# Convolution norm by streamed squares in channel layout, and q and k of head pair 1 by block products in a seventh front round

## What is computed

```python
h = rms_norm(x, g_pre_mix[l])
proj = jnp.einsum('bsd,dp->bsp', h, w_in[l])
hc, bg, cg, q, k, v = jnp.split(proj, 6, axis=-1)      # 512 columns each
y_conv = short_gated_conv(hc, bg, cg, w_conv[l])       # bg * conv3(cg * hc)
y_attn = chunked_band_attention(q, k, v, rel_bias[l])  # 8 heads of 64
y = jnp.concatenate([group_rms_norm(y_conv, g_conv_out[l], CONV_GROUPS),   # 8 groups of 64
                     group_rms_norm(y_attn, g_attn_out[l], N_HEADS)], axis=-1)
y = jnp.einsum('bsm,md->bsd', y, w_out[l])
x = x + rms_norm(y, g_post_mix[l])
# then a dense SwiGLU FFN with its own norms
```

## Time and profile before

| | us |
|---|---|
| median of 3 runs (1108.47 to 1108.7) | 1108.63 |
| the profiled execution's own time | 1108.71 |
| its span in the trace | 1106.7 |
| TensorE busy | 1096.9 (99%) |
| VectorE busy | 759.8 (69%) |
| ScalarE busy | 467.3 (42%) |
| front, 60.75 to 183.92 in the trace | 123.17 |
| attention, 183.92 to 367.22 | 183.30 |

### The profile page before, as it was taken

How to read it: one execution, slowest core, us unless ns; L and a number is a source line. 1 busy time by engine, 2 the same in 40 slices (tenths; PEclk the granted TensorE clock), 3 DMA queues, 4 the chain that set the end, 5 groups by cost and what they waited for, 6 DMA issues and landing times.

```text
span 1106.7 us, 15974 instructions
## 1 busy us (share of the span) xinstructions
PE 1096.9 (99%) x5653; PEld 909.5 (82%) x5653; DVE 759.8 (69%) x1206; ACT 467.3 (42%) x818; POOL 162.4 (15%) x258
## 2 busy tenths in 40 slices
PE   9999999999999999999999999999999999999997
PEld 7888888878888888888888888888888888888886
DVE  6878854354546656868787777878787786555584
ACT  6542333555555655734322232323223256444441
POOL 3300022010101220312112211211221110000031
PEclk9999999999999999999999999999999999999999
DMA  7332216300100444535546445543644689776632
GB/s 272 107 120 75 58 57 224 119 20 20 39 3 19 163 162 133 172 95 174 159 142 209 136 122 187 177 146 114 218 136 152 214 307 377 232 237 223 218 114 79
DMA packets 116182, 164.10 MB, mean 148 GB/s; under 512 B 7752, under 2 KB 73304, under 8 KB 116128
## 3 DMA queue, kind: packets, MB, share of 16 engines
q1 hardware_dynamic: 98496, 103.30, 29.3%
q0 software_dynamic: 16464, 55.89, 14.4%
q10 hardware_dynamic: 1168, 4.20, 1.0%
HBM read 119.56 MB, written 46.94 MB: 150 GB/s over the span
## 4 chain that ended last, share of the span: by engine, by line
PE 98%; ACT 1%; DVE 1%; DMA 0%; issue 0%; DVEq 0%; POOL 0%; POOLq 0%
PE psum L1278 34%; PE psum L1305 18%; PE psum L872 12%; PE psum L1111 10%; PE psum L1162 8%; PE psum L1023 4%; PE psum L915 3%; PE psum L896 2%; PE psum L886 2%; PE psum L861 1%; PE psum L999 1%; PE psum L923 0%; PE psum L1005 0%; PE psum L905 0%; ACT arena L1514 0%; PE psum L992 0%
## 5 line engine op out<-in xcount | busy, mean ns | idle before, releaser
L1278 PE MATMUL psum<-arena_r,ws 128*128 128x512 f32 x960 | 224.1, 389 | 0.0
L1278 PEld LDWEIGHTS psum<-arena_r,ws 128*128 128x128 f32 x960 | 180.3, 188 | 37.3
L1278 PE MATMUL psum<-hT,ws 128*128 128x512 f32 x720 | 169.9, 389 | 0.0
L1278 PEld LDWEIGHTS psum<-hT,ws 128*128 128x128 f32 x720 | 135.2, 188 | 27.9
L872 PE MATMUL psum<-hT,ws 128*128 128x512 f32 (+1 forms) x624 | 142.2, 380 | 0.6 <-ACT arena L1540 0.6
L1305 PE MATMUL psum<-hT 128*128 128x512 f32 (+1 forms) x600 | 135.2, 385 | 0.0
L1305 PEld LDWEIGHTS psum<-hT 128*128 128x128 f32 x600 | 111.3, 188 | 22.5
L872 PEld LDWEIGHTS psum<-hT,ws 128*128 128x128 f32 x624 | 107.9, 189 | 19.9 <-issue 0.8
L2408 DVE TENSOR_TENSOR misc<-misc,psum 128x512 f32<-128x512 f32 x100 | 68.6, 686 | 48.3 <-PE psum L1278 46.0
L1729 ACT ACTIVATE ws<-o_raw 128x512 fp32r<-128x512 f32 x40 | 25.1, 627 | 139.1 <-DVE o_raw L2386 138.6
L1162 PE MATMUL psum<-ws,hT 128*128 128x512 f32 x348 | 81.8, 393 | 0.0
(11 more groups left out here) (263 smaller groups left out, 1557.7 us busy)
## 6 DMA issues: line engine op xcount, KB each, us to landing
raw<-in_w_ffn_in SPq DMA_DIRECT2D x44, 512.0 KB, 4.2
act_scratch<-arena POOLq DMA_DIRECT2D x77, 256.0 KB, 3.2
raw<-in_w_in SPq DMA_DIRECT2D x22, 512.0 KB, 3.8
arena<-in_w_ffn_out POOLq DMA_DIRECT2D x22, 512.0 KB, 5.6
arena<-act_scratch SPq DMA_DIRECT2D x38, 256.0 KB, 3.3
arena<-in_x SPq DMA_DIRECT2D x16, 512.0 KB, 6.3
raw<-in_w_out SPq DMA_DIRECT2D x16, 512.0 KB, 3.4
raw<-act_scratch SPq DMA_DIRECT2D x26, 256.0 KB, 3.2
```

What stands on the lines that cost most here:

```text
L1278: last = mm(blocks(bank), w[:, k * P:(k + 1) * P], b_operand(i, part, k), start=fresh_bank and k == 0 and w is hi and part == 0, stop=k == ...
```

## The change

**The norm of rows 0 to 2.** The squares (ScalarE, `square_y`) are split into a high part in row `CR` and a low part in `CU` (`high_sq` on ScalarE, `low_sq` on VectorE). TensorE multiplies both with a stationary 128 x 128 matrix `same_head`, 1/64 inside a group's block, so that every channel of a group gets the group's mean in `PP[2]`, 128 x 1024, with no transposing: four matmuls of 512 columns a row (`stats`). ScalarE takes the logarithm with eps as bias and then the exponent of -1/2 of it (`conv_roots`), and VectorE sharpens that by one Newton step and multiplies the row (`mix_row`, four instructions of 1024 columns, the first two of which write PSUM). GpSimd, the spreading and the transposes are gone for these rows; row 3 keeps the old way. The tasks stand behind other products than before.

**q and k of pair 1.** `FRONT` becomes 7: round 5 makes q and k of pair 1, round 6 those of pair 0. Pair 1's are put into rows 18 and 17, where convolution rows 0 and 1 have been (`stage_c11`, `make_c22`, `make_c21` and a `bank_sum` write there, behind the stores of these rows), stored to DRAM and loaded back to rows 2 and 4 before attention needs them at (t = 0, s = 7). The chunks of plain projection go from 8 to 6, the pieces in attention from 61 to 45 besides the three ahead of it. `FILLS` spreads them anew, and the reading of halves and the splits follow it by computed tables (`halves_done`, `chunks_next`). The taps of convolution row 3 move from steps 3 and 4 of pair 3 to steps 1 and 2. The convolution rows come back from DRAM late in pair 3's time instead of before attention.

```diff
-    OUT0 = 2 * PAIRS
+    FRONT_PAIRS = 2
+    FILLED = 2 * (PAIRS - FRONT_PAIRS) + 2
+    OUT0 = FILLED
...
-    FRONT = 6
+    FRONT = 5 + FRONT_PAIRS
...
-        QN, KN = 13, 14
+        QK_ROWS = (None, (13, 14), (2, 4), (0, 1))
+        QK_STAGED = (18, 17)
...
-        FILLS = [[1] + [2] * 7 + [1]] * LAST + [[1] + [2] * 4 + [1] * 4]
+        FILLS = [[1, 2, 2, 2, 1, 1, 1, 1, 1]] * LAST + [[1] * 9]
...
+        CG, BG = FILLED - 2, FILLED - 1
+
+        def step_of(q):
+
+            return next((STEPS * t + s for t in range(PAIRS) for s in range(STEPS)
+                         if pieces_ahead(t, s) <= q < pieces_ahead(t, s) + FILLS[t][s]), -1)
+
+        def halves_done(t, s):
+
+            return [h for h in range(2 * FILLED) if step_of(4 * h + 3) == STEPS * t + s - 1]
+
+        def chunks_next(t, s):
+
+            return [g for g in range(2, FILLED) if step_of(8 * g - 9) == STEPS * t + s - 1]
...
+            def store_qk(n):
+
+                t = FRONT - 1 - n
+                for part, done in enumerate((c12_made, c21_made)):
+                    sp.wait_ge(done, n + 1)
+                    at = (2 * t + part) * P
+                    sp.dma_start(qk_d[at:at + P, :], row(QK_STAGED[part])).then_inc(qk_stored, 16)
+
...
+            for n in range(1, 7):
+                next_front(n)
             store_conv(0), store_conv(1)
-            sp.wait_ge(front_lo, split(FRONT - 1, 5))
-            load(1, win_d[:, :, o_k + P:o_k + 2 * P])
-            store_conv(2)
+            for n in range(7, FRONT):
+                next_front(n)
+                store_qk(n - 2)
+                if n == 7:
+                    store_conv(2)
+            for slot in range(2):
+                sp.wait_ge(front_lo, split(FRONT - 1, (3, 5)[slot]))
+                load_filled(slot)
+            store_qk(FRONT - 2)
+            if FRONT == 7:
+                store_conv(2)
             sp.wait_ge(v_stored[0], 32)
             sp.wait_ge(v_stored[1], 48)
...
+                if g == OUT0 + 1:
+                    sp.wait_ge(qk_ready, 2 * PAIRS)
+                    for t in range(PAIRS - 1):
+                        load_conv(t)
...
             def stats(t):
 
-                pe.wait_ge(conv_sq, t + 1)
-                if t == 0:
-                    pe.wait_ge(v_copied, NT)
-                else:
-                    pe.wait_ge(conv_var, t)
-                conv_stats(PP[3]).then_inc(conv_stat, 1)
-
-            def norms(t):
-
-                pe.wait_ge(conv_rs, t + 1)
+                pe.wait_ge(conv_mixed, means_split(t))
                 if t > 0:
-                    pe.wait_ge(conv_mixed, t)
-                conv_norms(PP[2], 0, NT).then_inc(conv_norm, 1)
-
-            behind = {(4, 1): (stats, 0), (4, 3): (stats, 1), (4, 4): (norms, 0),
-                      (5, 0): (norms, 1), (5, 1): (stats, 2), (5, 4): (norms, 2)}
+                    pe.wait_ge(conv_mixed, mixed(t - 1))
+                for half in range(2):
+                    for part in (CR, CU):
+                        last = mm(PP[2][:, half * HALF:(half + 1) * HALF], same_head, row_r(part)[:, half * HALF:(half + 1) * HALF],
+                                  start=(part == CR), stop=(part == CU))
+                last.then_inc(conv_stat, 1)
...
-                act.wait_ge(*((front_out, n) if n else (t_lo, NT)))
+                act.wait_ge(*((t_lo, NT) if n == 0 else (front_out, n) if n < 6 else (c12_made, n)))
                 go(u2, BANK[0], ACT.Copy).then_inc(p1_copied, 1)
+
+            def stage_c11(n):
+
+                act.wait_ge(prod, multiplied(n, 3))
+                if n == 5:
+                    act.wait_ge(conv_stored[0], 16)
+                else:
+                    act.wait_ge(qk_stored, 32 * (n - 5))
+                go(tiles_of(row(QK_STAGED[0]), 0), blocks(BANK[0]), ACT.Copy).then_inc(c11_done, 1)
 
...
+            def high_sq(t):
+
+                act.wait_ge(conv_sq, squared(t, 0))
+                if t == 0:
+                    act.wait_ge(consts_made, 6)
+                    go(same_head.rearrange("p (g d) -> p g d", d=HD),
+                       group[:, :].rearrange("p (g o) -> p g o", o=1).broadcast_to([P, 2, HD]), ACT.Copy, scale=1.0 / HD)
+                if t > 0:
+                    act.wait_ge(conv_mixed, mixed(t - 1))
+                go(row_r(CR), row(CU), ACT.Copy).then_inc(conv_sq, 1)
+
+            def conv_roots(t, bank):
+
+                act.wait_ge(conv_stat, t + 1)
+                go(row(CR), bank, ACT.Ln, bias=eps_col[:, 0:1]).then_inc(conv_root, 1)
+                act.wait_ge(conv_root, rooted(t) - 1)
+                go(row(CR), row(CR), ACT.Exp, scale=-0.5).then_inc(conv_root, 1)
...
-            front_copy_first(4), square_y(0)
-            front_high(5, 0), square_y(1), front_high(5, 1), front_high(5, 2), front_high(5, 3)
-            spread_conv(0), front_high(5, 4), spread_conv(1), front_high(5, 6)
-            front_copy_first(5), square_y(2), front_high(5, 5)
+            front_copy_first(4), square_y(0), high_sq(0)
+            for i in range(4):
+                front_high(5, i)
+            conv_roots(0, PP[2]), square_y(1), front_high(5, 4), high_sq(1), front_high(5, 5), front_high(5, 6)
+            front_copy_first(5), conv_roots(1, PP[2]), square_y(2)
+            for i in range(3):
+                front_high(6, i)
+            high_sq(2), stage_c11(5)
+            for i in range(3, 5):
+                front_high(6, i)
+            conv_roots(2, PP[2]), front_high(6, 5), front_high(6, 6)
+            for n in range(6, FRONT - 1):
+                front_copy_first(n)
+                for i in range(3):
+                    front_high(n + 1, i)
+                stage_c11(n)
+                for i in range(3, 7):
+                    front_high(n + 1, i)
+            front_copy_first(FRONT - 1)
 
             def first_chunk(g):
...
+            def low_sq(t):
+                dve.wait_ge(conv_sq, squared(t, 1))
+                tt(row_r(CU), row(CU), row_r(CR).bitcast(F32), ALU.subtract).then_inc(conv_mixed, 1)
+
+            def mix_row(t):
+
+                f, mean, y = row(CR), PP[2], row(CONV_ROWS[t])
+                dve.wait_ge(conv_root, rooted(t))
+                chain(stt(mean, mean, EPS, f, ALU.add, ALU.mult))
+                chain(stt(mean, mean, -0.5, f, ALU.mult, ALU.mult))
+                chain(stt(f, mean, 1.5, f, ALU.add, ALU.mult))
+                stt(y, y, params[:, t, 3:4], f, ALU.mult, ALU.mult).then_inc(conv_mixed, 1)
...
             make_u2(4)
             front_low(5, 0)
-            conv_stats_read(0)
+            low_sq(0)
             make_u3(4)
             front_s(5)
             front_low(5, 1)
@@ -2081,23 +2184,48 @@
             dve.wait_ge(prod, multiplied(4, 3))
             times(2, 0, BANK[0]).then_inc(c11_done, 1)
             front_low(5, 3)
+            mix_row(0)
             make_c22(4, tiles_of(row(CV), 1), 1)
-            conv_stats_read(1)
             front_low(5, 4)
+            low_sq(1)
             make_c21(4, tiles_of(row(CV), 0), 0)
-            conv_mix(0)
-            front_low(5, 6)
+            front_low(5, 5)
             make_c12(4)
             times(2, 1, u2).then_inc(front_out, 1)
-
-            make_u2(5)
-            conv_mix(1)
-            make_u3(5)
-            conv_stats_read(2)
-            front_low(5, 5)
+            front_low(5, 6)
+
+            for n in range(5, FRONT - 1):
+                q_row, k_row = [row(r) for r in QK_STAGED]
+                if n == 6:
+                    mix_row(2)
+                make_u2(n)
+                front_low(n + 1, 0)
+                if n == 5:
+                    mix_row(1)
+                make_u3(n)
+                front_s(n + 1)
+                front_low(n + 1, 1), front_low(n + 1, 2)
+                if n == 5:
+                    low_sq(2)
+                    dve.wait_ge(conv_stored[1], 16)
+                else:
+                    dve.wait_ge(qk_stored, 32 * (n - 5))
+                make_c22(n, tiles_of(k_row, 1), 1)
+                front_low(n + 1, 3), front_low(n + 1, 4)
+                make_c21(n, tiles_of(k_row, 0), 0)
+                front_low(n + 1, 5)
+                if n == 5:
+                    dve.wait_ge(conv_stored[0], 16)
+                bank_sum(n, 6, tiles_of(q_row, 1), blocks(u2), blocks(BANK[3]), c12_made)
+                front_low(n + 1, 6)
+
+            n = FRONT - 1
+            if FRONT == 7:
+                mix_row(2)
+            make_u2(n)
+            make_u3(n)
             low(1, 0, 0)
-            make_c22(5)
-            conv_mix(2)
+            make_c22(n)
             nc.vector.memset(gate[:, :], 0.0).then_inc(tile_free, 1)
             chain(nc.vector.memset(nmax[:, :], 0.0))
...
+            def drain(t, s):
+
+                for h in halves_done(t, s):
+                    if h // 2 >= CG:
+                        read_half(h // 2, h % 2)
+                        if h == 2 * CG + 1:
```

(3 more changed lines are left out.)

184 lines of the change are left out of this document (89 added, 95 removed).

## The result

The changed kernel takes 1122.47 us (median of 4, 1122.3 to 1122.77), the kernel before 1108.59 us in the same session: a ratio of 1.0126, with a 95% interval of 1.0108 to 1.0143. It is slower by 13.9 us, where the prediction had 1121.5 us, 12.9 us more. The profiled execution has a span of 1120.6 us against 1106.7, again 13.9.

What follows compares the result with a forecast made beforehand. TensorE, busy 99% of the span, was taken as the bound. Its work -8.06, front waits +12.4, pairs 0 to 2 +4.8, pair 3 +1.8 and clock +2.0 sum to +12.9 us: 1121.5 us, range 1113.5 to 1127.0.

Steps and rivals of the forecast that it cites:

- TensorE's work: Matmul work saved: -5.13 us in the norm and -2.93 in q and k of pair 1, together -8.06.
- The first wait: Front, before product (4,6): TensorE waits 7.0 us for `make_c22`, behind the root and `mix_row(0)`; 7.3 with the restart.
- the three waits: Front: TensorE waits 7.0 us before (4,6), 2.0 before (5,5), 2.5 before `stats(2)`; +12.4 with restarts.
- The restart of 0.3: Front, behind each wait: a run of twelve matmuls starting fresh takes 3.03 us instead of 2.74.
- The table loads: ScalarE's root in the front: two loads per row, six in all, at 1.28 us each.
- The clock: Front, behind the 7.0 us wait: TensorE may come back at 1.2 GHz, costing +2.0 us, bounds 0 and 4.
- Pairs 0 to 2: Attention: with fewer filler pieces TensorE waits 1.34 and 0.25 us in each pair, +4.8 us in all.
- Pair 3: Attention: earlier taps delay tile 2's exponents, 1.6 us, and the copy behind, about 0.2; +1.8, bounds 0 and 4.1.
- (a): Rival, front: the root is cheaper, table loads hide and the clock doesn't fall, gap 4.4 us; 1114.6 us, chance 0.11.
- (b): Rival, front: the root is dearer, a table load costing twice its row's price; 1126.6 us, chance 0.09.
- (c): Rival, front: VectorE gets to `make_c22` in time and round 5 has no waits; 1107.2 us, chance 0.07.
- (d): Rival, attention: bound by ScalarE everywhere, all 16 pieces taken out (22.1 us) turn into waiting; 1137 us, chance 0.02.

Runs made afterwards that it cites:

- old_norm_filled: `old_norm` with one filler piece moved from step 3 to step 7 in pairs 0 to 2, and pair 3's taps behind the bias additions: 1108.58 us.
- old_norm: Kernel before plus only q and k of pair 1 by block products in a seventh front round, norm of rows 0 to 2 as before: 1113.91 us.
- no_loads: Kernel after with the root's logarithm replaced by an exponential, so ScalarE loads no other table in the front (factors wrong): 1119.26 us.
- short_mix: Kernel after without the Newton step of rows 0 to 2, one VectorE instruction a row in place of four: 1113.13 us.
- fill_step7: Kernel after with one filler piece moved from step 3 to step 7 in pairs 0 to 2: 1119.54 us.
- squares_later: `old_norm_filled` with ScalarE's squares of tiles 0 and 1 in pair 3 taken at step 4 instead of step 3: 1108.49 us.
- taps_late: Kernel after with the taps of convolution row 3 in pair 3 back behind the bias additions, at steps 3 and 4: 1120.28 us.
- c22_first: Kernel after with `make_c22` for block (4,6) put ahead of `mix_row(0)` on VectorE instead of behind it: 1118.99 us.
- keep_busy: Kernel after with 24 more matmuls into an unread bank, put on TensorE between front blocks (4,5) and (4,6): 1121.8 us.

## Why the prediction was right, and where it was off

**TensorE's work.** -8.06 us: the norm's -5.13 and the products' -2.93. From one start to the next, the four new matmuls of a row take 0.91 us (148.15 to 149.06), as worked out; their row's 1.07 holds the way through the array, and so do the 2.88 of a product, which was taken at 2.74. `old_norm_filled`, the products with 2.8 us more of waiting and no change in time, agrees with the -2.93, and the 8.2 us between the profiled executions of `old_norm` and the kernel after agree with the -5.13.

**The first wait**, 7.0 us worked out, 6.70 measured. Its parts: the root 4.8 against 150.72 to 155.51, 4.79; `mix_row` 5.2 against 155.54 to 160.61, 5.07, since the three instructions on PSUM take 1.23 each, less than the 1.28 taken from the earlier trace rows. The method (laying the durations of before on the order of after) gave each of the three waits in its place: 7.0, 2.0, 2.5 against 6.70, 1.65, 2.50. The restart of 0.3 at each was hardly there: 2.98 for twelve in place of 2.88. The front lasts 150.4 us (60.75 to 211.15), where 151 was worked out.

**The table loads.** 1.28 us each, six of them, as the earlier trace rows. Shown by `no_loads`: 2.70 us for two, of which 0.02 is the exponential in place of the logarithm (1.10 and 1.12). The Trainium skill ("ScalarE: Activation LUTs", section "What ACT_TABLE_LOAD costs") counts 2.66 us a switch; here the measurement decides, and it is half of that. The same page's section on table sets has logarithm and exponent in one set; the compiled kernel makes no use of that and has a load for each.

**The clock.** +2.0 taken between 0 and 4; measured 2.34 at its place, 2.5 in the time. Right in kind and size. What I missed is that it isn't a term beside the chain but a part of it, because `stats(1)` waits behind the slow matmuls. For the sum of this kernel it makes no difference; for an edit that shortens the chain it does (`short_mix`). The Trainium skill ("TensorE: Matmul & The Clock Gate", part 1) lets the clock fall after idleness and rise after TensorE has been busy for a while; the rows of the first wait agree (1.00 until 159 us with TensorE idle since 154.66, 0.50 from 160 to 166, 1.00 from 167 on).

**Pairs 0 to 2.** 3 x (1.34 + 0.25) worked out, and these very numbers in the rows of all three pairs. The cause, a piece missing at step 7, is shown by `fill_step7`.

**Pair 3** is the term that was mis-sized: +1.8 predicted, 3.0 measured. I had 1.6 for the exponents of tile 2, which was 1.18, and 0.2 for "the copy behind it". That copy (L2276) does cost about 0.2: the transposes of `turn_back` start 0.93 behind those of tile 2 (350.72 to 351.65), 0.72 in the kernel before (336.16 to 336.88). For the second wait, `output`'s 1.81 us, I had no term at all. The step that failed is that the path ends with "about 0.2 more for the copy behind it": I followed VectorE's lateness to the next bias additions and not to its other customers. It also delays the sum of squares of the row, from there GpSimd's power and VectorE's scaling, and with that the place at which ScalarE squares tiles 0 and 1, and these squares stand ahead of the reading that `output` needs. In the kernel before they begin 1.05 us ahead of the transposes of that tile (340.03 and 341.08), in the kernel after 1.66 us behind them (356.16 and 354.50). That they are what the reading stands behind is shown by `squares_later`, where the reading is in time; the way back to VectorE is read from the rows, and `taps_late` bears it out for half of the wait. In the timeline of after:

```profile
351.41 2.90 POOL L772 TENSOR_TENSOR rst<-o_eps,mhalf 128x16 f32<-128x16 f32 x1 [40.25 <-DVE o_eps L2378]
...
354.34 1.22 DVE L2382 TENSOR_TENSOR arena<-o_raw,rst 128x1024 f32<-128x1024 f32 x1 [1.25 <-POOL rst L772]
...
355.65 0.42 DVE L2281 COPY o_raw<-psum 128x256 f32<-128x256 f32 x1
...
356.16 0.26 ACT L1630 ACTIVATE sq_junk<-o_raw 128x64 f32<-128x64 f32 x1 [2.22 <-issue]
...
357.74 1.00 ACT L1623 ACTIVATE arena<-psum 128x1024 f32<-128x1024 f32 x1
```

L772 is GpSimd's power, L2382 the scaling, L2281 the copy whose result L1630 squares, and L1623 the reading.

**The sum.** -8.06, waits of the front 10.85, clock and restarts 2.5, pairs 0 to 2 4.8, pair 3 3.0: +13.1 against 13.9 measured. Some 0.8 us of attention are in no wait. By the timeline it lasts 211.15 to 381.10, 169.95 us (the prediction had about 168). In the kernel before the same view has 183.75 to 367.15, 183.40, and 183.4 - 22.08 + 4.8 + 3.0 = 169.1. Step beside step, about half of the 0.8 lies in pairs 0 to 2, mostly where the waits of 0.25 are: that stretch is 1.03 shorter (4.01 to 2.98), where a piece less and the wait make 1.38 - 0.25 = 1.13. The other half lies in pair 3, with the 0.2 of the late copy. So the view of waits leaves out a tenth or two at such a place; no run tests it.

**The rivals.** (a) and (b) turned on the price of a load, which is the row's. What (a) had for it is there, but small: row 2's first load begins while TensorE is still at the means that the logarithm waits for (188.56; `stats(2)` is 188.34 to 189.54), so it doesn't wait for them. In row 0 it begins at 150.72, when ScalarE's instruction ahead of it has ended and the means are there already, so nothing is hidden. And a wait as short as (a)'s 4.4 us would hardly have kept the clock up: behind the 4.00 us in the profiled execution of `no_loads` it fell. (c), VectorE in time for `make_c22`, would have needed the 6.70 us to be nothing; `c22_first` shows that even with that wait gone 7 us of waiting remain in the front. (d) had all removed work turn into waiting; 7.8 of 22.1 us did.

## What to carry to other kernels

Work taken off the busiest engine is a gain only as long as its neighbours' chain fits into what is left. Lay the durations of the trace on the new order by hand and ask at each semaphore who comes last, following a late engine to all its customers: here that gave six of seven kinds of wait within 0.45 us, and the seventh, which had no term, is the customer that was not followed. A wait that sits in a chain moves when the order is changed, and goes only when the chain gets shorter.

Filler work is placed, not only counted. Taking a piece out of a step that was exactly covered costs what the piece covered, and moving one by a step can move what hangs on it.

## What the runs showed of the hardware

The price of idleness for TensorE isn't a matter of the last wait alone. In the profiled executions the matmuls behind waits of 6.70 and 4.00 us ran slow in each case seen (24 in 8.06 and 8.42 us, 12 in 5.46 us in place of 5.72 and 2.98); behind 2.92 and 3.06 us they did not (5.72; 1.19 for four). But behind the third wait of the front they took 1.20 and 5.62 us in the kernel after (wait 2.50), 1.82 and 6.64 in `keep_busy` (wait 2.48, the same wait of 1.65 ahead of it), and 1.20 and 7.21 in `no_loads` (wait 2.12, TensorE busy for 22.9 us ahead of it). An earlier fall doesn't decide it either: the clock had fallen at the first wait in the kernel after and in `no_loads`, and not in `keep_busy`. What does decide stays open.

Behind these short waits the clock fell only after TensorE had gone on. In `keep_busy` the matmuls begin again at 185.91, and the granted clock is 1.00 up to 186, 0.61 from 186 to 187, 0.50 up to 189, 0.68 from 189 to 190 and then 1.00. In `no_loads` they begin at 183.59, and it is 1.00 up to 184, 0.87 from 184 to 185, 0.50 up to 188.

The same kernel can differ from one execution to the next: `short_mix` has two executions 1.5 us longer than the other two, at a mean clock of 0.997 against 0.999, and `no_loads` one that is 2.5 us and more shorter, at 0.998 against 0.995. So "did not fall" above is said of one execution each. In `keep_busy`, filling the long wait gave 2.3 us and lost 1.6 of them again; here dummy matmuls paid only with every wait nearby filled (-2.5 us with 40 of them).

A table load took 1283 ns with no idle time of ScalarE ahead of it, six times in the front. Instructions of VectorE with one operand and the result in PSUM, 128x1024 in f32, took 1.23 us each; the last of `mix_row`, which is all in SBUF, took 1.28.
